# Subtracting the two softmaxes of a differential attention before the transposes, in a two-block transformer kernel

## The reference

```python
s = jnp.einsum('bhcqd,bhckd->bhcqk', qblk, kt).astype(jnp.float32) * scale   # 4 heads h, c = 0, 1
s = jnp.where(mask, s, -jnp.inf)                                             # causal
a = jax.nn.softmax(s, axis=-1)
w = a[:, :, 0] - lam * a[:, :, 1]
return jnp.einsum('bhqk,bhkv->bhqv', w.astype(vt.dtype), vt)                 # v is 128 wide
...
o = rms_norm_2(o, subln) * (1.0 - lambda_init)
```

## Time and profile before

| | |
|---|---|
| median of 3 runs | 2084.41 us (2080.0 to 2084.63) |
| the profiled execution's own time | 2080.16 us |
| its span, first to last instruction | 2078.1 us |
| PE busy | 2032.3 us, 98% |
| DVE busy | 1592.4 us, 77% |
| ACT busy | 1398.4 us, 67% |
| POOL busy | 178.5 us, 9% |
| mean granted TensorE clock | 0.995 |

### The profile page before, as it was taken

The page is one execution under the profiler, slowest core; times in us unless marked ns, Lnnn a source line. Parts: engine busy times, 40 slices in busy tenths (PEclk is TensorE's granted clock), DMA queues, the critical chain, the costliest instruction groups (busy, mean ns, idle before and its releaser), DMA issues.

```text
span 2078.1 us, 31845 instructions
## 1 busy us (share of the span) xinstructions
PE 2032.3 (98%) x10437; PEld 1684.3 (81%) x10437; DVE 1592.4 (77%) x1784; ACT 1398.4 (67%) x1896; POOL 178.5 (9%) x230
## 2 busy tenths in 40 slices
PE   7999999999999999799999999999999999999998
PEld 6888888888887877688888888888888888888877
DVE  4357643453687867889898989898989898989984
ACT  3258643222455446488888888888888888888863
POOL 0000000111000000111111111111111111110100
PEclk9999999999999999899999999999999999999999
DMA  6411024775355220499999999999999999999971
GB/s 202 147 62 62 21 77 147 252 274 177 126 188 194 84 89 29 170 381 384 372 382 370 379 366 380 369 373 371 378 371 382 370 378 372 372 375 370 374 254 41
DMA packets 97264, 543.79 MB, mean 262 GB/s; under 512 B 18365, under 2 KB 20777, under 8 KB 39594
## 3 DMA queue, kind: packets, MB, share of 16 engines
q1 hardware_dynamic: 77952, 497.07, 62.4%
q0 software_dynamic: 13744, 40.40, 6.4%
q10 hardware_dynamic: 5498, 5.39, 0.9%
HBM read 524.04 MB, written 35.01 MB: 269 GB/s over the span
## 4 chain that ended last, share of the span: by engine, by line
PE 90%; DVE 4%; ACT 2%; issue 2%; DMA 2%; ACTq 0%; POOL 0%; DVEq 0%
PE PS L2840 17%; PE PS L2841 17%; PE PS L2842 17%; PE PS L281 9%; PE PS L283 9%; PE PS L282 9%; PE PS L1156 2%; PE PS L2714 1%; PE PS L2850 1%; DMA AR<-c_oh 1%; PE PS L2095 1%; PE PS L1088 1%; PE PS L751 1%; PE PS L2833 1%; PE PS L2028 1%
## 5 line engine op out<-in xcount | busy, mean ns | idle before, releaser
L2708 DVE TENSOR_TENSOR WL<-RING,WH 128x2048 fp32r<-128x2048 f32 x385 | 872.9, 2287 | 97.2 <-ACT WH L2688 94.5
L2688 ACT ACTIVATE WH<-RING 128x1024 fp32r<-128x1024 f32 x770 | 801.9, 1058 | 160.2 <-PE PS L2842 153.4
L2840 PE MATMUL PS<-WH,RA 128*128 128x512 f32 x1540 | 610.1, 396 | 0.0
L2841 PE MATMUL PS<-WL,RA 128*128 128x512 f32 x1540 | 600.9, 390 | 0.0
L2842 PE MATMUL PS<-WH,RA 128*128 128x512 f32 x1540 | 600.7, 390 | 0.0
L2840 PEld LDWEIGHTS PS<-WH,RA 128*128 128x128 f32 x1540 | 289.5, 188 | 65.6 <-issue 7.9
L2842 PEld LDWEIGHTS PS<-WH,RA 128*128 128x128 f32 x1540 | 289.3, 188 | 61.7
L2841 PEld LDWEIGHTS PS<-WL,RA 128*128 128x128 f32 x1540 | 289.7, 188 | 57.4
L281 PE MATMUL PS<-WH,RA 128*128 128x512 f32 (+1 forms) x538 | 210.5, 391 | 3.1 <-issue 2.2
L283 PE MATMUL PS<-WH,RA 128*128 128x512 f32 (+1 forms) x538 | 207.2, 385 | 0.0
L282 PE MATMUL PS<-WL,RA 128*128 128x512 f32 (+1 forms) x538 | 207.1, 385 | 0.0
(11 more groups left out here) (413 smaller groups left out, 2267.1 us busy)
## 6 DMA issues: line engine op xcount, KB each, us to landing
RING<-w_experts SPq DMA_DIRECT2D x390, 1024.0 KB, 7.6
RING<-w_front SPq DMA_DIRECT2D x54, 1024.0 KB, 4.9
RING<-w_down_q POOLq DMA_DIRECT2D x5, 2048.0 KB, 8.3
sum_scr<-RING POOLq DMA_DIRECT2D x20, 512.0 KB, 4.8
RING<-sum_scr SPq DMA_DIRECT2D x8, 1024.0 KB, 5.1
RING<-w_front SPq DMA_DIRECT2D x5, 768.0 KB, 4.7
RING<-sum_scr SPq DMA_DIRECT2D x4, 768.0 KB, 4.7
AR<-bias_scr SPq DMA_DIRECT2D x132, 3.0 KB
```

The costliest lines, as they stand in the source:

```text
L2688: e.activation(WH[:, m % 3, v], RING[:, m % 6, v], ACT.Copy).then_inc(s("m_hi"), 1)
L2708: e.tensor_tensor(WL[:, m % 3, :], RING[:, m % 6, :], WH[:, m % 3, :].bitcast(F32), ALU.subtract).then_inc(s("m_lo"), 1)
L2840: e.matmul(PS[bank][:, :], lhs[0][:, kr + k, :], WH[:, m % 3, c], start=(not opened and kr == 0 and k == 0), stop=False)
L2841: e.matmul(PS[bank][:, :], lhs[0][:, kr + k, :], WL[:, m % 3, c], start=False, stop=False)
```

## The change

Both exponentials of a pair stay in PX2 until DVE has formed their weighted sum PW2 = PX2[0] + PX2[1] * (-lambda * sum0 / sum1) over the whole width. That one tile is transposed, copied and multiplied with the values, and one finish scales by 1 / sum0. The pipeline is written out by pairs: PE at step p does the logits of pair p, the fills, the transposes of pair p-2 and the values of pair p-3; DVE does the weights of pair p-1, the two reductions of pair p, and the finish of pair p-4. Each "between" is called with 2p and 2p+1 at the end of a step of ACT and DVE. Some of the places n in it are moved.

```diff
+        def dve_diff_weights(e, q):
+
+            m, w = 2 * q, diff_width(q)
+            e.wait_ge(s("a_ex"), UD + m + 2)
+            e.reciprocal(RI2[:, m:m + 2], RS2[:, m:m + 2]).then_inc(v_c.sem, v_c.up())
+            e.wait_ge(v_c.sem, v_c.n)
+            e.tensor_scalar(RI2[:, m + 1:m + 2], RI2[:, m + 1:m + 2], RS2[:, m:m + 1], LM[:, 5:6], ALU.mult, ALU.mult
+                            ).then_inc(v_c.sem, v_c.up())
+            if q >= 2:
+                e.wait_ge(s("p_t"), UD + q - 1)
+            e.wait_ge(v_c.sem, v_c.n)
+            e.scalar_tensor_tensor(PW2[q % 2][:, 0:w], PX2[1][:, 0:w], RI2[:, m + 1:m + 2], PX2[0][:, 0:w], ALU.mult, ALU.add
+                                   ).then_inc(s("v_pw"), 1)
...
+            for p in range(20):
+                if 1 <= p <= 16:
+                    dve_diff_weights(e, p - 1)
+                if p < 16:
+                    dve_diff_logits(e, 2 * p)
+                    dve_diff_logits(e, 2 * p + 1)
+                if p >= 4:
+                    dve_diff_finish(e, p - 4)
+                dve_diff_between(e, 2 * p)
+                dve_diff_between(e, 2 * p + 1)
...
+            for p in range(19):
+                for n in (2 * p, 2 * p + 1):
+                    if n < 32:
+                        w = diff_width(p)
+                        e.wait_ge(s("v_lg"), UD + n + 1)
+                        if p:
+                            e.wait_ge(s("v_pw"), p)
+                        e.activation(PX2[n % 2][:, 0:w], LG2[n % 2][:, 0:w], ACT.Exp, bias=NM2[:, n % 2:n % 2 + 1], scale=-1.0,
+                                     accum_out=RS2[:, n:n + 1]).then_inc(s("a_ex"), 1)
+                if 2 <= p < 18:
+                    q = p - 2
+                    w = diff_width(q)
+                    e.wait_ge(s("p_t"), UD + q + 1)
+                    if q >= 2:
+                        e.wait_ge(s("p_o"), UD + q - 1)
+                    e.activation(PT2[q % 2][:, 0:w], PS[T_B[q % 2]][:, 0:w], ACT.Copy).then_inc(s("a_pt"), 1)
+                act_diff_between(e, 2 * p)
+                act_diff_between(e, 2 * p + 1)
...
-            if n in (16, 24, 32):
-                pe_mx_T(e, (n - 16) // 8)
+            if n in (19, 27, 35):
+                pe_mx_T(e, (n - 19) // 8)
...
-            if n in (17, 25, 33):
-                act_mx_high(e, (n - 17) // 8)
+            if n in (21, 29, 37):
+                act_mx_high(e, (n - 21) // 8)
...
-            if n in (13, 21, 29, 35):
-                dve_mx_mean(e, (n - 13 + 2) // 8)
-            if n in (14, 22, 30):
-                dve_mx_norm(e, (n - 14) // 8)
-            if n in (18, 26, 34):
-                dve_mx_low(e, (n - 18) // 8)
+            if n in (16, 24, 32, 38):
+                dve_mx_mean(e, (n - 16 + 2) // 8)
+            if n in (17, 25, 33):
+                dve_mx_norm(e, (n - 17) // 8)
+            if n in (22, 30, 38):
+                dve_mx_low(e, (n - 22) // 8)
```

More of the change, by code:

```diff
@@ L1059, in out_part, with pe_attention @@
             return PS[O_B[m // share % 2]][:, 128 * q:128 * q + 128]
-        def pe_attention(e, u0, units, logits, values, PX, PT, first_free, between, both=0, share=1):
+        def pe_attention(e, u0, units, logits, values, PX, PT, first_free, between, share=1):
             N = len(units)
@@ L1066, in pe_attention @@
                 if n < N:
-                    if n >= 2 and not (both and n % 2):
-                        e.wait_ge(s("v_lg"), u0 + n - 1 + both)
+                    if n >= 2:
+                        e.wait_ge(s("v_lg"), u0 + n - 1)
                     else:
@@ L1071, in pe_attention @@
                             e.wait_ge(s(sem), v)
[L1072 to L1075, removed]
+                    logits(e, units[n], PS[S_B[z]]).then_inc(s("p_s"), 1)
                 between(e, n)
@@ L1720, in program @@
         PT2 = [WB[:, 2048 + 512 * n:2560 + 512 * n] for n in range(2)]
+        PW2 = [ar(12288 + 512 * n, 512) for n in range(2)]
         RS2 = AT2[:, 384:416]
@@ L2029, in diff_values @@
                              start=(j == 0), stop=(j == i))
[L2030 to L2034, removed]
[L2035 to L2050 removed]
+            x.then_inc(s("p_o"), 1)
@@ L2063, in program @@
         VX_F, VX_O = 16, 24
-        FILLED = [sum(FILL[:n + 1]) // 12 for n in range(len(FILL))] + [8] * (36 - len(FILL))
+        FILLED = [sum(FILL[:n + 1]) // 12 for n in range(len(FILL))] + [8] * (40 - len(FILL))
         def use_bank(kind, i):
@@ L2105, in pe_diff @@
             first_free.update({b: [("v_xt", XT["qk"] + QK_BANKS.index(b, 6) + 1)] for b in (2, 3)})
-            pe_attention(e, UD, DIFF, diff_logits, diff_values, PX2, PT2, first_free, pe_diff_between, both=1)
+            for p in range(19):
+                if p < 16:
+                    if p:
+                        e.wait_ge(s("v_lg"), UD + 2 * p)
+                    else:
+                        for b in S_B:
+                            for sem, v in first_free[b]:
+                                e.wait_ge(s(sem), v)
+                    diff_logits(e, DIFF[2 * p:2 * p + 2], [PS[b] for b in S_B])
+                pe_diff_between(e, 2 * p)
+                pe_diff_between(e, 2 * p + 1)
+                if 2 <= p < 18:
+                    q = p - 2
+                    e.wait_ge(s("v_pw"), q + 1)
+                    if q >= 2:
+                        e.wait_ge(s("a_pt"), UD + q - 1)
+                    else:
+                        for sem, v in first_free[T_B[q]]:
+                            e.wait_ge(s(sem), v)
+                    for j in range(DIFF[2 * q][0] + 1):
+                        x = e.transpose(PS[T_B[q % 2]][:, j * 128:(j + 1) * 128], PW2[q % 2][:, j * 128:(j + 1) * 128], IDT)
+                    x.then_inc(s("p_t"), 1)
+                if p >= 3:
+                    q = p - 3
+                    e.wait_ge(s("a_pt"), UD + q + 1)
+                    if q >= 2:
+                        e.wait_ge(s("v_fin"), UD + q - 1)
+                    diff_values(e, q)
         def act_mx_high(e, i):
```

45 lines of the change are left out of this document (32 added, 13 removed).

## The result

| | before | after |
|---|---|---|
| median (7 runs each) | 2081.84 us (2079.73 to 2084.63) | 2088.51 us (2086.29 to 2089.55) |
| ratio, 95% interval | | 1.0029 [1.0019, 1.0038] |
| profiled execution: own time, span | 2080.16, 2078.1 us | 2089.05, 2086.9 us |
| mean granted clock | 0.995 | 0.989 |
| first logits of the attention to the routing's product (L281) | 755.77 to 823.37: 67.60 us | 755.49 to 830.61: 75.12 us |

The change loses 6.7 us by the medians (8.8 by the spans of the two profiled executions). The change lies under 0.3% and can still be told from none: the interval excludes 1. PE has less to do and yet it takes longer; of the 8.8 us between the two profiled executions 7.5 lie between the attention's first logits and the routing's first product. Where the other 1.3 us come from was not followed up.

A forecast was written before the change was run, and what follows sets the result against it. PE bounds the attention up to pair 7, then a loop through DVE and ACT; 0.6 behind at the last exponential, 4.0 tail and 0.5 clock make 5.1 us longer, 2089.5 us from a median of 2084.41; range 2079 to 2096.

The forecast's parts named there:

- pair 7's logits: End of the attention's first regime, where PE is the bound: they start at 780.8 us for 784.12, a gain of 3.3 us.
- turn at 384, at 512: From pair 8 on, one turn of the loop through DVE and ACT: 2.9 us at 384 columns, 3.4 at 512.
- norm in pair 8, in pair 12: DVE stands still for POOL's power behind the mean, with the pair's weights queued behind: 1.8 us each, 3.6 in all.
- first half, second half: DVE's halves of the expert weights: 0.6 us in pair 10; 2.5 us in step 11, where DVE waits for ACT's.
- reduction of unit 30: The last pair's first reduction on DVE: at 817.4 us, from 788.9 plus 21.8 of turns plus 6.7 of waits.
- from there to the routing's product: The tail behind the last exponential: one chain of 9.2 us against 5.2 before, so 4.0 us longer.
- first rival: ACT and DVE overlap better in the loop than laid out: 4.7 us come back, 2084.8 us; chance 0.3.
- Clock: PE's clock may halve in the tail and double its work behind the norm: 0.5 us taken of a possible 0 to 2.5.
- second rival: The clock falls in the tail and again in the loop's gaps: 2093.9 us, slower; chance 0.25.
- the tail's terms: Sum read, weights, finishes, mean, norm, transposes, values and the third block's low part, last exponential to routing: summed as 9.2 us.
- the upper end of the range: 2096 us: the clock falls in tail and loop, with the weighted sum 0.05 us longer in 16 steps.
- the split at pair 7: Split of 2048 columns on ACT and DVE, behind pair 5's copy: gives 1 us back, leaving a lead of 2.3 us.

The follow-up runs named there:

- e9: Changed kernel with DVE forming each weighted sum a second time, behind a wait for the first: 2093.22 us, 1.0048 of the kernel before; stretch 81.96 us.
- e10: Changed kernel with 8 matmuls of a constant, never read, in PE's gaps in the tail only: 2087.22 us, 1.0022 of the kernel before; stretch 73.76 us.
- e4: Changed kernel with 32 matmuls of a constant, never read, in PE's gaps in pairs 8 to 17: 2085.48 us, 1.0021 of the kernel before; stretch 72.84 us.
- e5: Changed kernel with ACT's split of 2048 columns one place earlier (n = 13 for 14): 2085.38 us, 1.0017 of the kernel before; stretch 71.46 us.
- e6: Changed kernel with norms and DVE's second half later, ACT's split and the third block's low part earlier: 2077.46 us, 0.9979 of the kernel before; stretch 63.62 us.
- e1: Changed kernel with norms one pair behind their means and the block's transposes following: 2081.75 us, 1.0003 of the kernel before; stretch 68.82 us.
- e2: Changed kernel with DVE's second half of the expert weights at n = 24 for 23: 2085.17 us, 1.0017 of the kernel before; stretch 72.91 us.

## Why the prediction was right

2088.5 us were measured and 2089.5 forecast, with the loss at 6.7 us by medians and 5.1 forecast. That the time itself is met to 1 us is in part luck: the forecast stood on a median of 3 runs that is 2.6 us above the one of 7, and on that one it would have been 2086.9. Right as to cause, and one term too small. In the order of the prediction:

| step | forecast | after's trace |
|---|---|---|
| pair 7's logits | 780.8 | 780.42 |
| first reduction of pair 8 | 788.9 | 788.69 |
| weighted sum, 512 columns, to the next instruction | 0.67 | 813.97 - 813.28 = 0.69 |
| product with -lambda, to the next | 0.22 | 813.28 - 812.91 = 0.37 |
| turn at 384, at 512 | 2.9, 3.4 | 3.05, 3.54 |
| norm in pair 8, in pair 12 | 1.8, 1.8 | 1.6, 1.5 |
| first half, second half | 0.6, 2.5 | 0.4, 2.45 |
| reduction of unit 30 | 817.4 | 817.50 |
| last exponential | 818.8 | 818.95 |
| from there to the routing's product | 9.2, and 0.5 for the clock | 11.66 |
| routing's product | about 828 | 830.61 |

The steps of the reductions, from their starts at 788.69, 793.36, 796.41, 799.86, 805.36, 810.43, 813.97 and 817.50, are 4.67, 3.05, 3.45, 5.50, 5.07, 3.54 and 3.53 us. Above turns of 3.05 and 3.54 they leave 1.62 for the norm of pair 8, 0.40 and 2.45 for the halves and 1.53 for the norm of pair 12. The turns were 1.0 us too short in the sum, since a product that the next instruction waits for takes 0.15 more than I took, and the waits 0.7 too long; that they nearly cancel is luck too. That the loop is loose was the first rival: it isn't (e9).

The stretch grew by 7.5 us and not by 5.1. Of the difference 2.0 us lie in the tail, 0.15 in the last exponential, and 0.28 are the earlier start of after's attention in its trace. The term that was mis-sized is **Clock**: I took 0.5 us of a possible 0 to 2.5. In the tail the PE work behind the norm takes 823.76 to 829.03, that is 5.3 us, where I had 0.5 + 0.6 + 1.8 = 2.9; e10 measures the clock's part at 2.35 us, 1.85 more than I took. The reason that I gave for 0.5, that a part of this work waits anyway, was wrong: from the norm to the finish there is only PE in the chain. The other reason, that in no row of the attention had the clock fallen, was about a PE that stood 0.45 us of 10 still, and the change itself made the gaps. So part of the second rival came true: the clock falls three times, at 791.1, 808.2 and 821.9, and is back at 798.0, 815.0 and 828.7. In the loop it cost little, about 0.3 us by pair 15 (59.9 in e4 against 60.2), where that rival had 2.4: a PE with 2.3 us of work in a turn of 3.5 can double a part of it and still be waited for seldom. The Trainium skill (TensorE: Matmul & The Clock Gate, "Part 1: The HAM clock gate") says that the gate is throttled by default and that activity releases it; what its rule alone would give for the tail, half clock throughout, is what the trace of after shows from 821.9 to 828.7 us, all but the last 0.3 us of that work, with 0.50 in the window at 827.

Two sums of the prediction don't come out as they stand: the tail's terms add to 9.1 us and not 9.2, and the upper end of the range (2096) is 1.3 us above what its terms give (2093.9 and 16 times 0.05, 2094.7). Neither changes the account.

What I had not seen is how much the split at pair 7 cost as a wait and not as a delay: I had it in the sum, at the right time, but called it a thing to be paid. e5 shows that one place earlier it is nearly free. The same holds for the norms. Four places of woven work carry 11.5 us of the stretch (e6), more than the whole loss of 7.5; with them moved the kernel is 0.2% faster than the kernel before. That is not yet the worth of the change itself: the same moves were not tried on the kernel before, where DVE also waits 0.87 us for the split. What also stays open is how much of the 11.5 us comes from the low part's place alone, which I didn't run by itself; e1, e2 and e5 add up to 12.2.

## What to carry over

When an edit shortens the work of the engine that bounds a software pipeline, every hand-placed piece of side work on the other engines must be placed again, because its cover is gone: here waits of DVE for POOL's power, for ACT's half and for ACT's split were absent or short while PE was full, and cost 1.5 to 3.7 us each once the loop ran through DVE. In this kernel it paid each time to put a consumer one step behind its producer on another engine and not right behind it. And charge idle time on PE twice: once for the wait, and once for the matmuls behind it at half clock, above all in a tail where nothing else is in the chain.

## What the runs showed of the hardware

- In after the clock fell to 0.50 at 821.9 us, 0.4 us into a gap of 2.32 us (ahead of 823.76) that follows a gap of 1.73 us (ahead of 820.28) and eight value records, though neither gap is as long as the 3.59 us ahead of 806.72, behind which PE first worked on at a clock of 1.00, to fall at 808.2 in the next gap. In e1, with gaps of 1.93 and 0.99 us and some work between, it stayed at 1.00. So the longest gap by itself doesn't tell.
- Once fallen it came back while PE worked without a gap: from L2096 at 823.76 it took until 828.7, which is nearly the whole of a short tail.
- A product of [128 x 1] on DVE is 0.27 us long, but the instruction that waits for its result starts 0.37 to 0.38 behind its start. A chain of such small operations is priced by that distance, not by their durations.
- A few matmuls of a constant held the clock at 1.00, but cost what they delay: 0.98 us in e10, out of 2.35 gained. In e4 they held it with 32 matmuls over 42 us, for 2.3 us net.
